# FFN gate and up in a one-core fp32 kernel: three products of 256 columns against one of 512 and one of 256

## What is computed

```python
def swiglu(x, w_gate, w_up, w_down):
    return (jax.nn.silu(x @ w_gate) * (x @ w_up)) @ w_down
...
h = h + 0.5 * swiglu(rmsnorm(h, ffn_norm_a[i]), ffn_a_w_gate[i], ffn_a_w_up[i], ffn_a_w_down[i])
```

## Time and profile before

| | |
|---|---|
| median of 3 runs | 1891.41 us (1890.90 to 1891.53) |
| the profiled execution | 1891.29 us |
| its span, first to last instruction | 1889.5 us |
| matmuls | 11168, as many weight loads |
| feed-forwards | 4 of 22 blocks, 88 blocks in all |
| DMA | 483.69 MB |

### The profile page before, as it was taken

One profiled execution on the slowest core, in us unless ns is written; L12 is line 12 of the kernel. 1 busy time (PEld: TensorE's weight loads), 2 busy tenths in 40 slices (PEclk: granted clock), 3 DMA queues, 4 the chain that ended last, 5 costly groups with the idle time before them and its releaser, 6 DMA issues.

```text
span 1889.5 us, 29101 instructions
## 1 busy us (share of the span) xinstructions
PE 1747.4 (92%) x11168; PEld 1385.0 (73%) x11168; DVE 1286.6 (68%) x2398; ACT 912.5 (48%) x1906; POOL 317.3 (17%) x332
## 2 busy tenths in 40 slices
PE   9999999999999999899999999999988777777777
PEld 8999969999999999579999889975333222232222
DVE  6555787565766575986556887885967776766444
ACT  5443665444544453665344665634544344344333
POOL 1000004000000000030000000433433333333331
PEclk9999999999999999999999999999999999999999
DMA  7555426965465545225555444699999999999997
GB/s 296 190 179 194 146 75 156 264 255 185 167 201 179 190 146 172 79 83 186 191 178 179 148 132 137 198 371 415 422 421 422 421 421 422 421 421 422 421 421 313
DMA packets 95705, 483.69 MB, mean 256 GB/s; under 512 B 10528, under 2 KB 10784, under 8 KB 62544
## 3 DMA queue, kind: packets, MB, share of 16 engines
q0 software_dynamic: 38544, 275.25, 37.7%
q1 hardware_dynamic: 57024, 206.59, 32.5%
HBM read 477.34 MB, written 4.46 MB: 255 GB/s over the span
## 4 chain that ended last, share of the span: by engine, by line
PE 58%; DMA 15%; issue 11%; DVE 7%; POOL 6%; ACT 3%; POOLq 0%; SPq 0%; ACTq 0%; DVEq 0%
PE PS L549 16%; PE PS L551 16%; PE PS L550 16%; DMA WH<-uv,A 4%; PE PS L2281 3%; PE PS L2302 2%; DMA WL<-uv,A 2%; DMA raw<-uv,A 2%; DMA A<-uv,A 2%; DMA raw<-wst 2%; DVE WL L1054 1%; POOL raw L658 1%; DMA XH<-uv,A 1%; ACT WH L675 1%; DMA YL<-uv,A 1%
## 5 line engine op out<-in xcount | busy, mean ns | idle before, releaser
L1054 DVE TENSOR_TENSOR WL<-raw,WH 128x1024 fp32r<-128x1024 f32 (+2 forms) x372 | 447.6, 1244 | 79.7 <-ACT WH L675 79.4
L549 PE MATMUL PS<-XH,WH 128*128 128x256 f32 x1608 | 456.6, 284 | 3.0 <-DVE XL L1062 2.2
L550 PE MATMUL PS<-XL,WH 128*128 128x256 f32 x1608 | 452.3, 281 | 0.0
L551 PE MATMUL PS<-XH,WL 128*128 128x256 f32 x1608 | 452.2, 281 | 0.0
L675 ACT ACTIVATE WH<-raw 128x1024 fp32r<-128x1024 f32 (+2 forms) x372 | 369.2, 1042 | 43.3 <-PE PS L551 19.5
L549 PEld LDWEIGHTS PS<-XH,WH 128*128 128x128 f32 x1608 | 303.2, 189 | 6.0 <-issue 3.6
L550 PEld LDWEIGHTS PS<-XL,WH 128*128 128x128 f32 x1608 | 303.2, 189 | 0.2
L551 PEld LDWEIGHTS PS<-XH,WL 128*128 128x128 f32 x1608 | 303.1, 188 | 0.0
L997 ACT ACTIVATE A<-A,RTK 128x1 f32<-128x1 f32 x256 | 75.0, 293 | 298.0 <-DVE A L1697 296.6
L728 ACT ACTIVATE A<-A 128x256 f32<-128x256 f32 x88 | 36.7, 417 | 342.2 <-DVE A L1089 342.2
L549 PE MATMUL PS<-GH,WH 128*128 128x256 f32 x704 | 198.2, 282 | 1.1 <-DVE WL L1054 1.1
(11 more groups left out here) (331 smaller groups left out, 2942.6 us busy)
## 6 DMA issues: line engine op xcount, KB each, us to landing
raw<-wst SPq DMA_DIRECT2D x380, 512.0 KB, 4.5
vscr<-A POOLq DMA_DIRECT2D x1, 3072.0 KB, 37.3
raw<-wst SPq DMA_DIRECT2D x6, 384.0 KB, 3.5
A<-vscr POOLq DMA_DIRECT2D x1, 2048.0 KB, 22.2
C<-cst SPq DMA_DIRECT2D x1, 1236.5 KB, 10.4
hT<-xin SPq DMA_DIRECT2D x2, 512.0 KB, 5.3
A<-vscr POOLq DMA_DIRECT2D x1, 1024.0 KB, 11.3
A<-skt SPq DMA_DIRECT2D x1, 1024.0 KB, 6.4
```

The source lines that it names most:

```text
L549: pe.matmul(o, wh, xh, start=start, stop=False, skip_group_check=True)
L550: pe.matmul(o, wh, xl, start=False, stop=False, skip_group_check=True)
L551: return pe.matmul(o, wl, xh, start=False, stop=stop, skip_group_check=True)
L1054: dv.tensor_tensor(WL[:, m % SPL, 0:w], raw[:, i % RAW, 0:w], f32(WH[:, m % SPL, 0:w]), ALU.subtract).then_inc(s_lo, 1)
```

## The change

The high and the low part of an activation now lie in one tile, side by side for each chunk: `X2` and `Y2`, with `XH`, `XL`, `YH`, `YL` as views of it. For gate and up, a chunk is one matmul of the high weight with 512 columns (high input, low input) into a whole PSUM bank, and one of the low weight with the 256 high columns, added to the first half of that bank. So a block takes two banks for gate and two halves of each: blocks alternate between banks 0, 1 and banks 6, 7 (`GU`). The two halves of a bank are added on the way out: ACT copies the second halves of both banks to `GS`, DVE adds the first halves to it, and a second DVE instruction multiplies by the norm. PE waits in block 1, ahead of up, until the root has been read out of bank 7. Down and all other products stay as they were.

```diff
-        XH = sb("XH", [128, 8, T], F32R)
-        XL = sb("XL", [128, 8, T], F32R)
...
+        X2 = sb("X2", [128, 8, 2, T], F32R)
+        Y2 = sb("Y2", [128, 8, 2, T], F32R)
+        XH, XL = X2[:, :, 0, :], X2[:, :, 1, :]
+        YH, YL = Y2[:, :, 0, :], Y2[:, :, 1, :]
...
+        GU = ((0, 1), (6, 7))
...
# ACT, ffn
+                    ac.wait_ge(s_used, U("up", NF * i + f))
+                    ac.activation(GS[:, b], PS[:, GU[b][0]:GU[b][0] + 2, T:2 * T], ACT.Copy).then_inc(s_silu, 1)
                     ac.wait_ge(s_gs, NF * i + f + 1)
                     ac.activation(GS[:, b, 0, :], GS[:, b, 0, :], ACT.Silu).then_inc(s_silu, 1)
...
# DVE, ffn
                     dv.wait_ge(s_used, U("up", n - 1))
-                    dv.tensor_tensor(GS[:, b], PS[:, b, :].rearrange("p (a t) -> p a t", a=2),
-                                     RT[:, 1:2, :].broadcast_to([128, 2, T]), ALU.mult).then_inc(s_gs, 1)
-                    dv.wait_ge(s_silu, n)
+                    dv.wait_ge(s_silu, 2 * n - 1)
+                    own(dv.tensor_tensor(GS[:, b], PS[:, GU[b][0]:GU[b][0] + 2, 0:T], GS[:, b], ALU.add))
+                    own.wait()
+                    dv.tensor_tensor(GS[:, b], GS[:, b], RT[:, 1:2, :].broadcast_to([128, 2, T]), ALU.mult).then_inc(s_gs, 1)
+                    dv.wait_ge(s_silu, 2 * n)
...
# PE, ffn
+                def chunk(W, a, b, kc):
+
+                    w = slice(128 * kc, 128 * kc + 128)
+                    o = PS[:, GU[b][a], :]
+                    pe.matmul(o, W[a][0][:, w], PAIRED[p][:, kc].rearrange("p a t -> p (a t)"), start=kc == 0, stop=False,
+                              skip_group_check=True)
+                    return pe.matmul(o[:, 0:T], W[a][1][:, w], PAIRED[p][:, kc, 0, :], start=False, stop=kc == 7,
+                                     skip_group_check=True)
...
-                        opening(p, "gate", n, PS[:, b, 0:T], "up", n, PS[:, b, T:2 * T])
+                        W = [weights(name, n) for name in ("gate", "up")]
+                        for kc in range(8):
+                            pe.wait_ge(s_xl, 8 * p + kc + 1)
+                            done = [chunk(W, a, b, kc) for a in range(2)]
+                        done[0].then_inc(s_used, 1)
+                        done[1].then_inc(s_used, 1)
...
-                        gemm("gate", n, 0, 8, NORMED[p], PS[:, b, 0:T], x=(s_xl, 0) if n == 0 else None).then_inc(s_used, 1)
-                        gemm("up", n, 0, 8, NORMED[p], PS[:, b, T:2 * T]).then_inc(s_used, 1)
+                        W = [None, None]
+                        for a in range(2):
+                            if f == 1 and a:
+                                pe.wait_ge(s_rt, p + 1)
+                            W[a] = weights(("gate", "up")[a], n)
+                            for kc in range(8):
+                                if n == 0:
+                                    pe.wait_ge(s_xl, kc + 1)
+                                ins = chunk(W, a, b, kc)
+                            ins.then_inc(s_used, 1)
```

More of the change, by code:

```diff
@@ L271, in program @@
         XF = sb("XF", [128, 8, T])
-        XH = sb("XH", [128, 8, T], F32R)
-        XL = sb("XL", [128, 8, T], F32R)
-        YH = sb("YH", [128, 8, T], F32R)
-        YL = sb("YL", [128, 8, T], F32R)
+        X2 = sb("X2", [128, 8, 2, T], F32R)
+        Y2 = sb("Y2", [128, 8, 2, T], F32R)
+        XH, XL = X2[:, :, 0, :], X2[:, :, 1, :]
+        YH, YL = Y2[:, :, 0, :], Y2[:, :, 1, :]
         GH = sb("GH", [128, 2, T], F32R)
@@ L483, in program @@
         NORMED = (X, X, Y, X, X, X, X, Y)
+        PAIRED = [X2 if v is X else Y2 for v in NORMED]
+        GU = ((0, 1), (6, 7))
         NORMED_FREE = (0, U("up", 21), U("uv", 1), U("mla_o", 7), U("up", 65), U("vsw", 3), U("up", 87), U("upab", 7))
@@ L510, in program @@
         last = {i % RAW: n for n, i in enumerate(where["pq"])}
-        rows = [(flat(XH[:, :, :]), (s_used, U("wout", 7)), 0), (flat(XL[:, :, :]), (s_used, U("wout", 7)), 0),
+        halves = [[v[:, 4 * k:4 * k + 4].rearrange("p a b c -> p (a b c)") for k in range(2)] for v in (X2, Y2)]
+        rows = [(halves[0][0], (s_used, U("wout", 7)), 0), (halves[0][1], (s_used, U("wout", 7)), 0),
                 (ROW0, (s_sbp, 4), 0), (ROW1, (s_sbp, 4), 0)]
-        rows += [(flat(w[:, :, :]), queried(SPLIT_PQ - 1), 0) for w in (YH, YL)]
+        rows += [(w, queried(SPLIT_PQ - 1), 0) for w in halves[1]]
         rows += [(flat(w[:, 2 * k:2 * k + 2, :]), queried(SPLIT_PQ - 1), 0) for w in (WH, WL) for k in range(2)]
```

## The result

The kernel with the change takes 1897.68 us (median of 7 runs, 1895.88 to 1898.41) against 1891.41 of the kernel before beside it (7 runs, 1890.50 to 1894.21): a ratio of 1.0029, 95% interval 1.0020 to 1.0039. The medians are 6.3 us apart; by the ratio, which is used from here on, the change costs 5.5 us (3.8 to 7.4). That is inside the predicted range, but 3.4 us above the predicted time and past the 0.2%, on a side that was given 0.30. The profiled execution took 1895.88 us, its span 1893.9 us. Its mean granted clock is 0.995; that of the kernel before is 0.991, so the clock was not granted in full throughout, as the prediction read the page, but it is 1.00 in the feed-forwards of both.

What follows compares the result with a forecast made beforehand. PE, busy 92% of the span and paced by columns nearly alone, was taken as the bound, with DVE and ACT chains at feed-forward ends. Terms -4.3 + 5.4 + 1.8 = +3.0 us on 1891.29 gave 1894.3 us, range 1887.5 to 1899.

Steps and rivals of the forecast that it cites:

- the 0.2%: Whole kernel: 3.8 us, about what a measurement can tell from no change; the bound lies at 1895.2 us.
- Ends: End of each feed-forward: the longer chain is bare there, 1.35 us each, +5.4 us in four ends.
- First blocks: First block of each feed-forward: the add isn't hidden by the reciprocal; 0.61 + 0.24 + 0.24 + 0.72 = +1.8 us.
- the later wait there: Second feed-forward, fifth block: PE's 1.06 us wait for late down weights, forecast to grow by 0.72 us.
- PE: Gate and up: 3.3 ns less per chunk, 53 ns per block, -4.3 us over 80 blocks.
- the 2 ns at which the prediction was to fall: Gate and up: the forecast falls if a chunk saves less than 2 or more than 6 ns.
- I cost all that at nothing: Middle blocks: weight splits, SP's loads and PE's bank wait come up to 1.35 us later, taken as hidden, 0 us.
- cover of nine tiles: SP's loads into `raw`: nine tiles, three blocks, ahead, said to hide a delay of up to 1.35 us.
- Nothing saved per chunk: Rival, gate and up: PE's block stays at 8.52 us and the chain is paid, 1898.5 us; chance 0.17.
- Weight loads: Rival, gate and up: weight loads set PE's pace, so 16 fewer per block give time back, 1885.6 us; chance 0.12.
- Hidden ends: Rival, feed-forward ends: something else ends the wait, so the ends cost nothing, 1888.8 us; chance 0.07.
- DVE as the bound: Rival, middle blocks: only 0.59 us of DVE's idle time left, blocks run over, 1902 us; chance 0.04.

Runs made afterwards that it cites:

- the experiments with blocks of 8.49 us: Changed kernel with first and last blocks in the old form (three products of 256, one multiply): 1891.08 us; changed kernel without copy and add: 1888.20 us.
- the long chain alone: The kernel before, with its 24 products per gate, given ACT's copy and a DVE add of the same shape: 1901.17 us, ratio 1.0051.
- the split product: The changed kernel with its 512-column product as two of 256 into the halves of the same bank: 1902.80 us, ratio 1.0054.
- the kernel with 128 columns: The changed kernel with the low-weight product as two of 128 columns, 16 more weight loads in a block: 2037.55 us, one run.
- the kernel without the add: The changed kernel without copy and add, only the first halves of both banks multiplied out of PSUM: 1888.20 us, ratio 0.9984.

## Why the prediction was right or wrong

- **Ends: right in place and size.** +5.4 was forecast and +5.42 measured, and the earlier trace rows had named each wait that would move. One part was off: the hand-off from ACT to DVE, taken as 0.04 like that from DVE to ACT, is 0.10 to 0.11, so the chain grew by 1.42, not 1.35. The third end grew by only 1.14, from 6.61, where it was 0.3 us longer than the first two; that brought the sum back to the forecast, by luck.
- **First blocks: right in three.** 0.61, 0.24 and 0.24 were forecast, 0.62, 0.24 and 0.24 measured. The stall of 0.19 in the second was left to the later wait there, which would have taken it in if the late unit had not moved as well.
- **PE: right in mechanism, mis-sized.** "I take 3.3 ns, since both paces are measured": it was 2.5 ns in three feed-forwards, and 1.7 in the second and in the experiments with blocks of 8.49 us, which is less than the 2 ns at which the prediction was to fall. The two paces of 118.3 and 233.3 ns (by which an instruction adds 3.3 ns, not "3 ns or less") were those of unbroken streams, and a difference of 1% of them was carried over to a stream that alternates. There, from start to start, the 512-column product takes 234.4 to 234.7 ns and the low-weight product 118.3 to 118.8. The term was -4.3 us and came to -2.7: -2.14 in three feed-forwards, and -0.5 in the second, whose +1.12 hold 1.64 of waits. The Trainium skill (TensorE: Matmul & The Clock Gate, Back-to-back issue gap) has, in its formula for a matmul by itself, a constant of 2.5 ns. The middle blocks of three feed-forwards of the changed kernel give just that, the second one less, while the formula's levels for 256 and 512 columns, 109.2 and 215.8 ns, are no more met here than before.
- **The step that failed: "I cost all that at nothing", for SP's loads behind DVE's splits.** The cover of nine tiles that was named for it holds in three feed-forwards and is already used up in the second, where the prediction itself had seen a unit land late. It moved the chain ahead of down there by 0.72 (measured 0.76), and held the landing of the unit fixed. The unit moved too, by 0.85, and gate's wait of 0.21 became 1.09. That is 0.88 us that was in no term. That the first block's chain delays it by way of the split that frees SP's tile fits the order of events: counted from the first down, that split and SP's next issue come 0.6 us later after the change. It fits the kernels too: with the long chain in the first block the unit comes 29.8 to 30.1 us behind the first down in all three (the changed one, the long chain alone, the split product), with the old chain 29.2 to 29.5 in five of six (the kernel with 128 columns, whose blocks are longer, is left aside). The sixth, the kernel without the add, has 29.94 and contradicts it as sole cause. What else moves the landing stays open; POOL's write, behind which it falls each time, is an untested candidate.
- **The sum**, by the stretches, missed by 2.7 us: 1.6 of PE's pace, 0.9 of the late unit and 0.2 of the second first block, all to the slow side. The forecast's middle lay 0.8 us under the bound, and either of the first two carried it over. With the middle of a forecast so near a bound, the chance beyond it should have been nearly as large as that within; it was 0.09 of 0.60.
- **Rivals.** Nothing saved per chunk gave 1898.5, close to the measured time, but for a wrong reason: the split product shows the saving. Weight loads do not bind: 16 loads less in a block gave 2.5 ns each. The Trainium skill (Perfetto Trace Analysis, Identifying the Most-Contended Engine) takes the load's busy share, beside the rate of arithmetic reached, as the measure of how near PE is to its limit. Here that share was 100% where loads didn't bind, and 93% (74.40 of 80.00 us) in the kernel with 128 columns, where their floor of 109 to 112 ns did. Hidden ends fell with the 1.29 us wait, DVE as the bound with the 0.52 us that are left to it.

## What to carry to other kernels

Joining two matmuls into one of twice the columns saves the fixed part of one instruction, here 1.7 to 2.5 ns of 118; adding the halves up again costs a copy and an add in each block, 1.42 us. That was free in the middle blocks, where DVE had 1.99 us of idle time to give, and fell due in ends and first blocks, where the pipeline drains and fills, so count ends against blocks, here 1.42 us against 27 to 40 ns, before making such a trade. A wait that is already bare in the profile has no cover left: move everything that feeds it by the change's delay, its DMAs too.

## What the runs showed of the hardware

- Two products of 128 columns, each with its own load of 128x128 fp32r weights, took 223 ns together, where one of 256 took 118: the two start 60 ns apart, but the loads 109 to 112.
- Recorded weight loads, 188 ns long each and overlapping, fill the time whether or not they set the pace; the distance from start to start is the only row that told.
- Waking DVE from ACT took 0.10 to 0.11 us (copy to add), waking ACT from DVE 0.04.
- With a write of 3072 KB under way, a unit of 512 KB took 27.0 us from issue to landing, where the median is 4.5.
